# Down projection of a decoder layer: where its sums are computed, what is kept for the fourth product, and in which order its activations are loaded

## The chip, the cores and the metric

One core of one Trainium2 chip runs the whole kernel. The metric is device time in microseconds; the number of a kernel is the median of its runs. TensorE (PE in the rows) multiplies, with its weight loads listed as PEld; VectorE is DVE, ScalarE is ACT, GpSimd is POOL, and SyncE (SP) issues nearly all DMA transfers.

## The reference, cut to what matters

One decoder layer over 1024 prompt tokens and 64 sample tokens (8 sequences of 8), all in float32. The part that the change touches:

```python
    up, ffn_state = causal_dwconv(rms_norm(x, g_pre_ffn) @ w_up, ffn_prev, w_conv_f, b_conv_f)
    gate, val = jnp.split(up, 2, axis=-1)
    x = x + rms_norm((jax.nn.gelu(gate) * val) @ w_down, g_post_ffn)
    e = (p @ w_ple) * jax.nn.sigmoid(rms_norm(x, g_ple_gate) @ w_ple_gate)
    x = x + rms_norm(e, g_post_ple)
```

with d_model 1024, d_ff 2816 and a PLE width of 256. F = gelu(gate) * val is 1088 tokens by 2816 channels and w_down 2816 by 1024. Ahead of this lie the short convolution and the stick-breaking attention, which stay as they are.

## The kernel before

**Precision.** A float32 product is made of three products of rounded parts: every operand tile is rounded by ScalarE (the high part, `*oph`), VectorE subtracts that from the tile (the remainder, `*opl`), and TensorE adds high x high, low x high and high x low in PSUM.

**Seven products for eight.** For the prompt tokens F is cut into four blocks: 11 and 12 are the first 512 tokens with channels 0 to 1407 and 1408 to 2815, 21 and 22 the same of the last 512 tokens. w_down is cut alike. The kernel computes seven block products where the plain way has eight, with sums of blocks as operands. On the side of F these are S1 = 21 + 22, S2 = S1 - 11, S4 = 12 - S2 and S3 = 22 - S2; on the side of the weights T3 (22 - 12), T2 (11 + T3), T4 (21 - T2) and T1 (22 - T2). They are computed tile by tile, 128 x 512 each, in place: S1 over 21, S2 and later S3 over 11, S4 over 12, T2 over the 11 weights kept in `w1`.

**Steps.** Each product runs over k = 0 to 10 (KF = 11 tiles of 128 channels). Step s = 11 n + k is tile k of product n, so there are 77 steps (DSTEPS); the order of the products is 11 x 11, 12 x 21, S2 x T2, S3 x T3, 22 x T4, S1 x T1, S4 x 22. A step is four blocks of 128 tokens with three matmuls of 512 columns each (L3264 to L3266). In products 0, 1, 5 and 6 (steps 0 to 21 and 55 to 76) it also has two sampled matmuls ahead of the others (L3249 and L3250), with `fs`, the rounded sample columns of F.

**Order of the work.** Every engine works through its own list in order and waits on semaphores. ScalarE's loop over s from 5 has `w_high(s)`, `f_high(s)` and, at certain s, other work: `fs_high(1)` (rounds the second half of the sample columns, tile `fsraw`) at s = 7, the copies out of PSUM after products 0 and 1 at s = 12 and 23, the rounding of the gate weights (`gate_high`) at s = 60 to 62, 65, 66, and for k = 5 to 7 after the loop. VectorE's loop has `w_low(s)` and `f_low(s)` with T3's two differences and `s4_sum`, and `summed` (PSUM sums at the end of a product) at s = 34, 45, 56 and 67. The rounded tiles lie in 4 buffers for weights (NWOP) and 3 for F (NFOP): `w_high(s)` waits for the end of step s - 4, `f_high(s)` for that of step s - 3. GpSimd computes S1, S2, S3, T2, T4, T1, the remainders of the gate weights and of the PLE weights. Weight tiles arrive in a ring of 5 buffers (NR); `down_rows(s)` waits until the remainder of the tile before in its buffer is done.

T3 is computed twice: at s = 22 + k as a difference of two loaded tiles, from which T2 is made, and for product 3 as T2 minus the 11 weights, loaded a second time.

**Loads of F.** F doesn't fit into SBUF while it is made; each of its 22 channel tiles is spilled to DRAM by `spill`, and `f_group(j)` reads groups of tiles back (F_GROUPS); a group waits until the group three before it has landed. Groups with a channel tile above 17 wait for its spill (`f_landed`). SP issues all of these and the weights in one list:

```python
            down_rows(6)
            f_group(6)
            hold(d_f, 23)
            spill(21, 1)
            down_rows(7)
            hold(p_st, NFF + 1)
            f_landed(21)
            f_group(7)
```

Of the kernel before, what the change touches and what calls it, by code (L numbers as in the profile page):

```python
# [124 lines left out]
def block_end(n, b):  # L125
# [62 lines left out]
def build(nc, inp, out, gate_spill, x1_spill, x2_spill, f_spill):  # L188
    with ExitStack() as ctx:
# [136 lines left out]
        w1 = [at(f"w1_{k}", [P, HALF], 190464 + T * k if k < 3 else R2 + 32768 + T * (k - 3)) for k in range(KF)]  # L326
        wd = [at(f"wd{j}", [P, HALF], R3 + T * j if j < 4 else 67584) for j in range(NR)]
# [199 lines left out]
        g_t1, T1_0 = g_t, 4 * NFF  # L527
        g_sa, SA0 = g_s1, 4
        g_sb, SB0 = g_s, 4
        g_sc, SC0 = g_foldm, 1  # L530
        d_sd, SD0 = d_cg, NFF
        d_td, TD0 = d_cw, 2 * NFF
# [89 lines left out]
        def _(sp):  # L622
# [261 lines left out]
            def down_rows(s):  # L884

                n, k = divmod(s, KF)
                if s >= NR:
                    if 2 * KF <= s - NR < 3 * KF:
                        hold(g_t1, T1_0 + s - NR - 2 * KF + 1)
                    else:  # L890
                        hold(d_dl, s - NR + 1)
                row_, h = ((k, 0), (KF + k, 0), (KF + k, 1), (k, 0), (KF + k, 0), (KF + k, 1), (KF + k, 1))[n]
                sp.dma_start(w1[k][:, :] if n == 0 else wd[s % NR][:, :], down_block(row_, h)).then_inc(wd_in[s % NR], 16)
                if n == 2:
                    if k >= 3:
                        hold(g_t1, T1_0 + k - 2)
                    sp.dma_start(wd12[k % 3][:, :], down_block(k, 1)).then_inc(w12_in[k % 3], 16)
# [26 lines left out]
            f_group(6)  # L924
# [87 lines left out]
        def _(pool):  # L1012
# [121 lines left out]
            def down_sum(s):  # L1134

                n, k = divmod(s, KF)
                w, b = w1[k][:, :], wd[s % NR][:, :]
                if n == 2:
                    pool.wait_ge(d_td, TD0 + k + 1)
                    g.tensor_tensor(w, w, b, ALU.add).then_inc(g_t1, 1)  # L1140
                    return
                pool.wait_ge(wd_in[s % NR], 16 * (s // NR + 1))
                pool.wait_ge(g_t1, T1_0 + k + 1)
                minus(b, b, w).then_inc(g_t1, 1)

            for k in range(KF):
                a11, a21, a22 = (fa[q][k][:, :] for q in ("11", "21", "22"))
                for q in ("21", "22"):
                    j, n = F_LANDED[q, k]
                    pool.wait_ge(f_in[j], F_IN0[j] + n)  # L1150
                g.tensor_tensor(a21, a21, a22, ALU.add).then_inc(g_sa, 1)
                pool.wait_ge(g_sa, SA0 + k + 1)
                pool.wait_ge(d_fl, k + 1)
                minus(a11, a21, a11).then_inc(g_sb, 1)
            def s3_sum(k):

                a11, a22 = fa["11"][k][:, :], fa["22"][k][:, :]
                pool.wait_ge(d_sd, SD0 + k + 1)
                pool.wait_ge(d_fl, 2 * KF + k + 1)
                minus(a11, a22, a11).then_inc(g_sc, 1)  # L1160

            for k in range(KF):
                down_sum(2 * KF + k)
                if k in (6, 9):
                    s3_sum(k // 7)
            for k in range(2, KF):
                s3_sum(k)
            for s in range(4 * KF, 6 * KF):
                down_sum(s)

            for k in range(KD):
                h, l = wgate[k]
                pool.wait_ge(a_gh, k + 1)
                minus(l[:, :], wraw[k][:, :], f(h)[:, :]).then_inc(g_wl, 1)
# [6 lines left out]
        def _(act):  # L1181
# [549 lines left out]
            def w_high(s):  # L1731
# [1660 lines left out]
```

## Time and profile before

| | us |
|---|---|
| median of 3 runs (1720.69 to 1721.9) | 1721.71 |
| the profiled execution, its time | 1724.81 |
| the profiled execution, its span | 1723.1 |
| TensorE busy in the span | 1692.3 |
| VectorE busy | 1106.5 |
| ScalarE busy | 782.2 |
| GpSimd busy | 439.9 |

The down projection lies between 1331.0 and 1590.9 us of the span. All times of rows are from this one execution, counted from the start of the span. An engine's share of busy time is a mean over stages of different kind, and idle time of an engine that others don't wait for costs nothing. A matmul's duration overlaps the next one's: matmuls of 512 columns of 0.39 us begin every 0.23 us.

### The profile page before, as it was taken

Reading aid. Unit: us, or ns where it says so; the run is one execution under the profiler, and the core shown is the slowest. Engines: PE = TensorE matmul, PEld = TensorE weight load, DVE = VectorE, ACT = ScalarE, POOL = GpSimd, SP = SyncE. Lnnn points to the kernel's source line nnn. Section 1 sums busy time; section 2 is a strip of 40 time slices with the busy share of each in tenths; the row PEclk is TensorE's granted clock in tenths of the full one; section 3 lists DMA queues with packets and bytes.
Section 4 is the critical chain, followed back from the end, with each engine's and each line's share of the span. In section 5 each row is a group of like instructions: output and inputs, shape, how many; then the busy total and the mean of one; then the engine's idle time right before and its main releaser. Section 6 shows DMA issues by size and latency. Waiting matters only on the chain.

```text
span 1723.1 us, 27761 instructions
## 1 busy us (share of the span) xinstructions
PE 1692.3 (98%) x9376; PEld 1474.3 (86%) x9376; DVE 1106.5 (64%) x1481; ACT 782.2 (45%) x1402; POOL 439.9 (26%) x337
## 2 busy tenths in 40 slices
PE   8999999999999999999999999999999798999998
PEld 7989998999899989988888888888888586887886
DVE  6265145325523647648688888888887779787566
ACT  6345244434534443235454444444444243465665
POOL 1000000000000000003365555555563726451200
PEclk9999999999999999999999999999999899999999
DMA  5312221231123115343222222222224842344343
GB/s 170 102 53 71 85 71 52 68 99 51 61 81 85 43 56 183 127 171 123 66 85 77 77 76 74 73 75 73 72 70 141 287 152 81 118 140 170 120 132 116
DMA packets 178184, 173.56 MB, mean 101 GB/s; under 512 B 16383, under 2 KB 144731, under 8 KB 178076
## 3 DMA queue, kind: packets, MB, share of 16 engines
q1 hardware_dynamic: 167130, 167.30, 30.3%
q10 hardware_dynamic: 10946, 4.91, 1.0%
q8 instruction: 57, 0.93, 0.2%
q14 instruction: 51, 0.42, 0.1%
HBM read 132.54 MB, written 39.62 MB: 100 GB/s over the span
## 4 chain that ended last, share of the span: by engine, by line
PE 90%; DVE 5%; issue 2%; DMA 1%; ACT 1%; SPq 1%; DVEq 0%; ACTq 0%
PE pair L3052 11%; PE pair L2747 9%; PE pair L2749 9%; PE pair L2748 9%; PE pair L3112 8%; PE pair L3114 8%; PE pair L3113 8%; PE pair L2701 5%; PE pair L3264 3%; PE pair L3266 3%; PE pair L3265 3%; PE pair L3121 2%; PE pair L2923 2%; PE pair L2893 2%; PE pair L2678 2%; PE pair L2676 2%
## 5 line engine op out<-in xcount | busy, mean ns | idle before, releaser
L2747 PE MATMUL pair<-xh,wh 128*128 128x384 f32 (+1 forms) x952 | 324.7, 341 | 0.0
L2749 PE MATMUL pair<-xh,wl 128*128 128x384 f32 (+1 forms) x952 | 311.2, 327 | 0.0
L2748 PE MATMUL pair<-xl,wh 128*128 128x384 f32 (+1 forms) x952 | 310.5, 326 | 0.0
L1048 POOL TENSOR_TENSOR srow<-hn,hn 128x512 f32<-128x512 f32 x8 | 12.0, 1506 | 814.1 <-DVE hn L2293 813.8
L2747 PEld LDWEIGHTS pair<-xh,wh 128*128 128x128 f32 x952 | 179.2, 188 | 4.3 <-issue 2.3
L2748 PEld LDWEIGHTS pair<-xl,wh 128*128 128x128 f32 x952 | 179.3, 188 | 0.0
L2749 PEld LDWEIGHTS pair<-xh,wl 128*128 128x128 f32 x952 | 178.7, 188 | 0.0
L3264 PE MATMUL pair<-woph,foph 128*128 128x512 f32 x308 | 123.3, 400 | 8.3 <-DVE fopl L2432 5.9
L3266 PE MATMUL pair<-woph,fopl 128*128 128x512 f32 x308 | 121.4, 394 | 0.0
L3265 PE MATMUL pair<-wopl,foph 128*128 128x512 f32 x308 | 121.3, 394 | 0.0
L1400 ACT ACTIVATE keep<-pair,bias 128x512 f32<-128x512 f32 (+4 forms) x100 | 58.2, 582 | 125.7 <-DVE pair L2146 53.6
L1960 DVE TENSOR_TENSOR wl<-raw,wh 128x1024 fp32r<-128x1024 f32 x48 | 58.8, 1224 | 75.3 <-ACT wh L1207 74.9
L2432 DVE TENSOR_TENSOR fopl<-f,foph 128x512 fp32r<-128x512 f32 x77 | 90.7, 1178 | 16.4 <-ACT foph L1761 16.3
L1761 ACT ACTIVATE foph<-f 128x512 fp32r<-128x512 f32 x77 | 48.4, 628 | 94.3 <-PE pair L3266 90.0
L3264 PEld LDWEIGHTS pair<-woph,foph 128*128 128x128 f32 x308 | 58.6, 190 | 26.2 <-issue 6.8
L2146 DVE TENSOR_TENSOR pair<-pair,far 128x128 f32<-128x128 f32 x64 | 15.1, 293 | 85.9 <-PE pair L2893 85.5
L3266 PEld LDWEIGHTS pair<-woph,fopl 128*128 128x128 f32 x308 | 58.6, 190 | 12.5
L3265 PEld LDWEIGHTS pair<-wopl,foph 128*128 128x128 f32 x308 | 58.7, 191 | 11.7
L3112 PE MATMUL pair<-bh,tch 128*128 128x512 f32 x168 | 67.2, 400 | 0.0
L3112 PE MATMUL pair<-bh,adh 128*128 128x512 f32 x168 | 65.5, 390 | 0.7 <-DVE uv L2393 0.7
L3114 PE MATMUL pair<-bh,tcl 128*128 128x512 f32 x168 | 65.6, 391 | 0.0
L3113 PE MATMUL pair<-bl,tch 128*128 128x512 f32 x168 | 65.6, 390 | 0.0
(409 smaller groups left out, 4394.3 us busy)
## 6 DMA issues: line engine op xcount, KB each, us to landing
rawp<-in_w_up SPq DMA_DIRECT2D x88, 256.0 KB, 3.8
raw<-in_w_in SPq DMA_DIRECT2D x80, 256.0 KB, 3.2
wd<-in_w_down SPq DMA_DIRECT2D x66, 256.0 KB, 2.8
f_spill<-cv SPq DMA_DIRECT2D x22, 552.0 KB, 2.8
f<-f_spill SPq DMA_DIRECT2D x44, 256.0 KB, 5.6
gat<-gate_spill SPq DMA_DIRECT2D x16, 544.0 KB, 4.5
x_spill<-x SPq DMA_DIRECT2D x16, 512.0 KB, 2.9
gate_spill<-stg SPq DMA_DIRECT2D x32, 192.0 KB, 1.9
```

Source lines behind the costliest of these rows:

```text
L2432: v.tensor_tensor(fop[s % NFOP][1][:, :], fa[F_OF[s // KF]][s % KF][:, :], f(fop[s % NFOP][0])[:, :], ALU.subtract).then_inc(d_fl, 1)
L2701: return t_.transpose(b, src, ident[0:rows, 0:rows])
L2747: t_.matmul(b, h, xhi, start=(k == 0), stop=False, skip_group_check=True)
L2748: t_.matmul(b, h, xlo, start=False, stop=False, skip_group_check=True)
L2749: ins = t_.matmul(b, l, xhi, start=False, stop=(k == KD - 1), skip_group_check=True)
L3052: ins = t_.matmul(o[:, 512 * c:512 * c + 512], x, w(t, c), start=first and i == 0, stop=last and i == 2, skip_group_check=True)
L3112: t_.matmul(o, w, x, start=n in "1675" and k == 0, stop=False, skip_group_check=True)
L3113: t_.matmul(o, w, xlow, start=False, stop=False, skip_group_check=True)
L3114: ins = t_.matmul(o, wlow, x, start=False, stop=k == KH - 1, skip_group_check=True)
L3264: t_.matmul(o, xh_[:, cols], w[0][:, :], start=n in (0, 2, 3, 5) and k == 0, stop=False, skip_group_check=True)
L3265: t_.matmul(o, xh_[:, cols], w[1][:, :], start=False, stop=False, skip_group_check=True)
L3266: ins = t_.matmul(o, xl_[:, cols], w[0][:, :], start=False, stop=k == KF - 1, skip_group_check=True)
```

## The change

All S and T sums and the remainders of the gate weights are computed by VectorE, at places of its loop that are written out; GpSimd keeps the remainders of the PLE weights. T3 is written to tiles of its own, `w3`, when it is first computed, and product 3 reads it there; the second load of the 11 weights for it falls away (`load_of` numbers the loads that are left). The groups of F are ordered anew: the 12 tiles 0 to 2 and then the second `fsraw` are the first that are read after the last spill, and the 21 and 22 tiles from 4 on come after the 12 tiles. The last three gate tiles are rounded inside the loop (s = 74 to 76), with `gate_low(7)` ahead of the last PSUM sums.

```diff
-F_GROUPS = ([[("11", k) for k in range(4)], [("11", k) for k in range(4, 8)], [("s", 0)], [("11", k) for k in range(8, KF)]]
-            + [[(q, k) for k in (2 * i, 2 * i + 1) for q in ("21", "22")] for i in range(3)]
-            + [[("12", k) for k in range(4)]]
-            + [[(q, k) for k in (2 * i, 2 * i + 1) for q in ("21", "22")] for i in range(3, 5)]
-            + [[("12", k) for k in range(4, 8)], [("21", KF - 1), ("22", KF - 1), ("s", 1)], [("12", k) for k in range(8, KF)]])
+F_GROUPS = [[("11", k) for k in range(4)], [("11", k) for k in range(4, 8)], [("s", 0)], [("11", k) for k in range(8, KF)],
+            [(q, k) for k in (0, 1) for q in ("21", "22")], [(q, k) for k in (2, 3) for q in ("21", "22")],
+            [("12", k) for k in range(3)], [("s", 1)], [("12", k) for k in range(3, 7)], [("12", k) for k in range(7, KF)],
+            [(q, k) for k in (4, 5) for q in ("21", "22")], [(q, k) for k in (6, 7) for q in ("21", "22")],
+            [(q, k) for k in (8, 9, 10) for q in ("21", "22")]]
+def load_of(s):
+    return s if s < 3 * KF else s - KF
...
@@ SyncE, the list of loads
-            f_group(6)
             hold(d_f, 23)
             spill(21, 1)
             down_rows(7)
             hold(p_st, NFF + 1)
             f_landed(21)
+            f_group(6)
+            hold(d_fs, DFS0 + 1)
             f_group(7)
             down_rows(8)
             f_group(8)
             down_rows(9)
+            down_rows(10)
             f_group(9)
-            down_rows(10)
+            down_rows(11)
             f_group(10)
-            down_rows(11)
-            hold(d_fs, DFS0 + 1)
+            down_rows(12)
             f_group(11)
-            down_rows(12)
+            down_rows(13)
             f_group(12)
-            for s in range(13, DSTEPS):
-                down_rows(s)
-                if s == 51:
+            for s in range(14, DSTEPS):
+                if s // KF != 3:
+                    down_rows(s)
+                if s == 49:
                     hold(p_dn, EACH * 4)
                     sp.dma_start(pn[:, 0:BLK, :], pp).then_inc(p_in, 16)
...
@@ GpSimd: down_sum, the S1 and S2 loop, s3_sum and the gate remainders fall away
+            pool.wait_ge(g_wl, KD)
             for k in range(2):
                 pool.wait_ge(a_eh, EH0 + k + 1)
                 minus(wl[k][:, :], raw[k][:, :], f(wh[k][:, :])).then_inc(g_wl, 1)
...
@@ ScalarE, at the end of its loop
+                if s >= 74:
+                    gate_high(s - 69)
             x2_high(1)
-            for k in range(5, KD):
-                gate_high(k)
...
@@ VectorE, the new functions (s1_sum, s3_sum, s4_sum and gate_low are of the same form)
+            def s2_sum(k):
+                dve.wait_ge(d_s1, S1_N + k + 1)
+                dve.wait_ge(d_fl, k + 1)
+                v.tensor_tensor(fa["11"][k][:, :], fa["21"][k][:, :], fa["11"][k][:, :], ALU.subtract).then_inc(d_s2, 1)
+            def t3_sum(k):
+                l = load_of(2 * KF + k)
+                dve.wait_ge(wd_in[l % NR], 16 * (l // NR + 1))
+                dve.wait_ge(w12_in[k % 3], W12_IN0 + 16 * (k // 3 + 1))
+                v.tensor_tensor(w3[k][:, :], wd[l % NR][:, :], wd12[k % 3][:, :], ALU.subtract).then_inc(d_t3, 1)
+            def t2_sum(k):
+                dve.wait_ge(d_t3, T3_N + k + 1)
+                v.tensor_tensor(w1[k][:, :], w1[k][:, :], w3[k][:, :], ALU.add).then_inc(d_t, 1)
+            def t41_sum(s):
+                l = load_of(s)
+                dve.wait_ge(wd_in[l % NR], 16 * (l // NR + 1))
+                b = wd[l % NR][:, :]
+                v.tensor_tensor(b, b, w1[s % KF][:, :], ALU.subtract).then_inc(d_t, 1)
...
@@ VectorE, its loop
             for s in range(5, DSTEPS):
                 if 0 <= s + 3 - 2 * KF < KF:
-                    weights_apart(s + 3 - 2 * KF)
-                if 0 <= s + 2 - 3 * KF < KF:
-                    t3_sum(s + 2 - 3 * KF)
+                    t3_sum(s + 3 - 2 * KF)
+                if 0 <= s + 2 - 2 * KF < KF:
+                    t2_sum(s + 2 - 2 * KF)
+                if 0 <= s + 1 - 3 * KF < KF:
+                    s3_sum(s + 1 - 3 * KF)
+                if 4 * KF <= s + 2 < 6 * KF:
+                    t41_sum(s + 2)
                 w_low(s)
                 f_low(s)
+                if s in (9, 10, 11, 12):
+                    s1_sum(s - 9)
+                    s2_sum(s - 9)
+                if 14 <= s < 21:
+                    s1_sum(s - 10)
+                    s2_sum(s - 10)
                 if KF <= s - 1 < 2 * KF:
                     s4_sum(s - 1 - KF)
...
+                if 61 <= s < 64:
+                    gate_low(s - 61)
+                if s in (66, 67):
+                    gate_low(s - 63)
+                if s >= 75:
+                    gate_low(s - 70)
             x2_low(1)
+            gate_low(KD - 1)
             summed(6, lambda b: y_half(b, 1), lambda b: y_half(b, 1))
```

## Rows read from the trace of the kernel before

**Rows 1.** The page: span, and busy time of each engine.
```profile
span 1723.1 us, 27761 instructions
...
PE 1692.3 (98%) x9376; PEld 1474.3 (86%) x9376; DVE 1106.5 (64%) x1481; ACT 782.2 (45%) x1402; POOL 439.9 (26%) x337
```

**Rows 2.** Stages: us, busy PE, PEld, DVE, ACT, POOL, then clock, DMA share, GB/s.
```profile
1341.99:1356.78 14.79, 13.66 (x58) 10.20 (x57) 14.79 (x10) 3.91 (x7) 14.48 (x10) 1.00 0.85 300
1356.78:1375.66 18.88, 9.23 (x30) 6.84 (x28) 7.71 (x8) 4.43 (x8) 14.02 (x11) 0.73 0.79 269
1375.66:1416.92 41.26, 41.26 (x183) 34.17 (x182) 32.99 (x44) 18.78 (x34) 11.70 (x7) 1.00 0.44 141
1416.92:1433.24 16.32, 16.32 (x73) 13.52 (x72) 15.63 (x17) 8.13 (x15) 10.65 (x7) 1.00 0.51 161
1433.24:1457.23 23.99, 19.17 (x74) 13.84 (x72) 23.99 (x21) 7.24 (x12) 17.26 (x11) 0.93 0.15 45
1457.23:1481.71 24.48, 24.48 (x110) 20.28 (x108) 21.41 (x29) 10.51 (x18) 7.92 (x5) 1.00 0.36 108
1481.71:1487.62 5.91, 5.69 (x26) 4.43 (x25) 5.17 (x9) 2.31 (x4) 2.58 (x2) 1.00 0.17 46
...
1552.48:1557.36 4.88, 3.44 (x15) 2.55 (x14) 4.88 (x10) 1.15 (x2) 0.00 (x0) 1.00 0.16 54
```

**Rows 3.** The long stand: waits, TensorE, chain, SP, landings of fsraw and spills, full DMA.
```profile
ACT fs L1769 <- DMA fsraw<-f_spill: 16.8, 1, 16.8
...
1369.99 0.80 PE L3249 MATMUL pair<-woph,fs 128*128 128x512 f32 x1 [9.65 <-DVE wopl L2427]
...
1342.09 5.30 DMA f_spill<-cv
...
1358.87 0.45 SPq L876 DMA_DIRECT2D fsraw<-f_spill  x1
...
DMA to landing us min/median/max: 5.8/7.3/8.7
...
f_spill<-cv SPq DMA_DIRECT2D x22, 552.0 KB, 2.8
...
1353.00:1364.00 11.00, 7.34 (x31) 5.21 (x29) 4.27 (x3) 0.00 (x0) 10.69 (x9) 1.00 1.04 387
```

**Rows 4.** VectorE and GpSimd in order of time: together, then each alone.
```profile
1339.59 2.40 DVE L2369 TENSOR_TENSOR cv<-cg,cv 128x1104 f32<-128x1104 f32 x1
...
1350.39 1.78 DVE L2427 TENSOR_TENSOR wopl<-w,woph 128x512 fp32r<-128x512 f32 x1
1352.09 1.78 DVE L2432 TENSOR_TENSOR fopl<-f,foph 128x512 fp32r<-128x512 f32 x1
...
1351.70 1.62 POOL L1048 TENSOR_TENSOR f<-f,f 128x512 f32<-128x512 f32 x1
...
1457.41 0.67 DVE L2479 TENSOR_TENSOR wd<-w,wd 128x512 f32<-128x512 f32 x1
1458.01 0.68 DVE L2427 TENSOR_TENSOR wopl<-wd,woph 128x512 fp32r<-128x512 f32 x1
...
1482.21 1.29 POOL L1048 TENSOR_TENSOR wd<-wd,w 128x512 f32<-128x512 f32 x1 [1.53 <-DMA wd<-in_w_down]
```

**Rows 5.** VectorE: a dependent pair, and F's remainder at an undisturbed step.
```profile
1331.82 1.36 DVE L2356 SCALAR_TENSOR_TENSOR cg<-ug,fw,cg 128x1104 f32<-128x1104 f32 x1
1333.22 1.37 DVE L2358 SCALAR_TENSOR_TENSOR cg<-ug,fw,cg 128x1104 f32<-128x1104 f32 x1
...
1395.57 0.69 DVE L2432 TENSOR_TENSOR fopl<-f,foph 128x512 fp32r<-128x512 f32 x1 [1.28 <-ACT foph L1761]
```

**Rows 6.** A remainder of 1024 columns, the last PSUM sums, the first gate matmul.
```profile
L1960 DVE TENSOR_TENSOR wl<-raw,wh 128x1024 fp32r<-128x1024 f32 x48 | 58.8, 1224 | 75.3 <-ACT wh L1207 74.9
...
1589.30 2.51 DVE L2464 TENSOR_TENSOR y<-pair,y 128x512 f32<-128x512 f32 x4
...
1590.91 0.62 PE L3052 MATMUL pair<-wgh,x2h 128*128 128x512 f32 x2
```

More of the change, by code:

```diff
@@ L326, in build @@
         w1 = [at(f"w1_{k}", [P, HALF], 190464 + T * k if k < 3 else R2 + 32768 + T * (k - 3)) for k in range(KF)]
+        w3 = [at(f"w3_{k}", [P, HALF], R1 + 33792 + T * k if k < 8 else 56320 + T * (k - 8)) for k in range(KF)]
         wd = [at(f"wd{j}", [P, HALF], R3 + T * j if j < 4 else 67584) for j in range(NR)]
@@ L526, in build @@
         a_eh, EH0 = a_dh, DSTEPS
[L527 to L532, printed above, removed]
+        d_s1, S1_N = g_s1, 4
+        d_s2, S2_N = g_s, 4
+        d_s3, S3_N = g_foldm, 1
+        d_s4, S4_N = d_cg, NFF
+        d_t3, T3_N = d_cw, 2 * NFF
+        d_t, T_N = g_t, 4 * NFF
         a_u2, U2_0 = a_snap, NFF
@@ L886, in down_rows @@
                 n, k = divmod(s, KF)
[L887 to L893, printed above, removed]
+                l = load_of(s)
+                if l >= NR:
+                    before = l - NR if l - NR < 3 * KF else l - NR + KF
+                    hold(*((d_t3, T3_N + before - 2 * KF + 1) if before // KF == 2 else (d_dl, before + 1)))
+                row_, h = {0: (k, 0), 1: (KF + k, 0), 2: (KF + k, 1), 4: (KF + k, 0), 5: (KF + k, 1), 6: (KF + k, 1)}[n]
+                sp.dma_start(w1[k][:, :] if n == 0 else wd[l % NR][:, :], down_block(row_, h)).then_inc(wd_in[l % NR], 16)
                 if n == 2:
                     if k >= 3:
-                        hold(g_t1, T1_0 + k - 2)
+                        hold(d_t3, T3_N + k - 2)
                     sp.dma_start(wd12[k % 3][:, :], down_block(k, 1)).then_inc(w12_in[k % 3], 16)
@@ L1132, in _ @@
             states_out(i5.at(), 1)
[L1134 to L1174, printed above, removed]
+            pool.wait_ge(g_wl, KD)
             for k in range(2):
@@ L2425, in w_low @@
                 dve.wait_ge(a_dh, s + 1)
-                src = w1[s % KF] if s // KF in (0, 2) else wd[s % NR]
+                n, k = divmod(s, KF)
+                src = w1[k] if n in (0, 2) else w3[k] if n == 3 else wd[load_of(s) % NR]
                 v.tensor_tensor(wop[s % NWOP][1][:, :], src[:, :], f(wop[s % NWOP][0])[:, :], ALU.subtract).then_inc(d_dl, 1)
@@ L2464, in summed @@
                     v.tensor_tensor(out_(b), down_bank(n, b), add(b), ALU.add).then_inc(d_dn, 1)
-            def weights_apart(k):
-                dve.wait_ge(wd_in[(2 * KF + k) % NR], 16 * ((2 * KF + k) // NR + 1))
-                dve.wait_ge(w12_in[k % 3], W12_IN0 + 16 * (k // 3 + 1))
-                b = wd[(2 * KF + k) % NR][:, :]
-                v.tensor_tensor(b, b, wd12[k % 3][:, :], ALU.subtract).then_inc(d_td, 1)
-            def t3_sum(k):
-                s = 3 * KF + k
-                dve.wait_ge(wd_in[s % NR], 16 * (s // NR + 1))
-                dve.wait_ge(g_t1, T1_0 + k + 1)
-                b = wd[s % NR][:, :]
-                v.tensor_tensor(b, w1[k][:, :], b, ALU.subtract).then_inc(d_td, 1)
@@ L2481, in s4_sum, with s1_sum @@
-            def s4_sum(k):
-                dve.wait_ge(g_sb, SB0 + k + 1)
-                dve.wait_ge(d_fl, KF + k + 1)
-                a12 = fa["12"][k][:, :]
-                v.tensor_tensor(a12, a12, fa["11"][k][:, :], ALU.subtract).then_inc(d_sd, 1)
+            def s1_sum(k):
+                for q in ("21", "22"):
+                    j, n = F_LANDED[q, k]
+                    dve.wait_ge(f_in[j], F_IN0[j] + n)
+                v.tensor_tensor(fa["21"][k][:, :], fa["21"][k][:, :], fa["22"][k][:, :], ALU.add).then_inc(d_s1, 1)
@@ new lines, in s2_sum, with s4_sum, s3_sum @@
+            def s2_sum(k):
+                dve.wait_ge(d_s1, S1_N + k + 1)
+                dve.wait_ge(d_fl, k + 1)
+                v.tensor_tensor(fa["11"][k][:, :], fa["21"][k][:, :], fa["11"][k][:, :], ALU.subtract).then_inc(d_s2, 1)
+            def s4_sum(k):
+                dve.wait_ge(d_s2, S2_N + k + 1)
+                dve.wait_ge(d_fl, KF + k + 1)
+                v.tensor_tensor(fa["12"][k][:, :], fa["12"][k][:, :], fa["11"][k][:, :], ALU.subtract).then_inc(d_s4, 1)
+            def s3_sum(k):
+                dve.wait_ge(d_s4, S4_N + k + 1)
+                dve.wait_ge(d_fl, 2 * KF + k + 1)
+                v.tensor_tensor(fa["11"][k][:, :], fa["22"][k][:, :], fa["11"][k][:, :], ALU.subtract).then_inc(d_s3, 1)
@@ L2488, in p_low, with gate_low @@
+            def gate_low(k):
+                dve.wait_ge(a_gh, k + 1)
+                v.tensor_tensor(wgate[k][1][:, :], wraw[k][:, :], f(wgate[k][0])[:, :], ALU.subtract).then_inc(g_wl, 1)
             def p_low(i):
```

10 lines of the change are left out of this document (6 added, 4 removed).

## The prediction

> **What bounds the kernel now.** I read the page first: TensorE is busy for 1692.3 of 1723.1 us and VectorE for 1106.5 [rows 1], so only TensorE's waits and the spans in which its clock falls can be won. The change touches the down projection alone, so I went to the table of stages there, with borders where steps begin [rows 2]. The reader should first look for stages in which nothing disturbs TensorE. Steps 9 to 21 took 41.26 us, 3.174 us each (a step of the sampled products); steps 22 to 27 took 16.32 us, 2.72 us each (a step without sample columns). Against these two rates the other stages are too long by:
> - steps 3 to 6: 14.79 - 4 x 3.174 = 2.09 us;
> - steps 7 and 8: 18.88 - 2 x 3.174 = 12.53 us;
> - steps 28 to 33: 23.99 - 6 x 2.72 = 7.67 us;
> - steps 43 and 44: 5.91 - 2 x 2.72 = 0.47 us;
> - step 66: 4.88 - 3.174 = 1.71 us.
>
> Together 24.47 us. Steps 34 to 42 run at the full rate, and what is left of the stage (turns, the ends of products) stays as it is.
>
> Next, what ends these waits. For steps 7 and 8 the view of waits has ScalarE idle for 16.8 us until the second fsraw lands [rows 3]. The SP rows say why it is late: SP waits for the last spill (issued 1342.09, 5.30 us on its way), then issues several groups, and fsraw only at 1358.87, the 25th transfer since 1342; it lands 8.7 us later. ScalarE's loop is strictly in order, and fs_high(1) stands in it at s = 7, so steps 8 and 9 can't be prepared. TensorE stands for 9.65 us until 1369.99, and then its sampled matmul takes 0.80 us where 0.39 is usual: the granted clock of the stage is 0.73, a mean over full speed and the lower level of 1.2 GHz after the long stand [rows 2, 3]. From landing to TensorE's next matmul are 2.4 us.
>
> For the other stages the reader lays VectorE's rows beside GpSimd's [rows 4]. While GpSimd sums, its operation takes 1.62 us or more (alone: 1.29), and VectorE's takes 1.78 us, one begun every 1.70 us. While GpSimd stands still, VectorE's takes 0.68 us, one begun every 0.60 us. The two alternate as if they shared a way to the data. In steps 3 to 6 VectorE has two remainders a step: 2 x 1.70 = 3.40 us, more than the 3.174 us of the step. In steps 28 to 33 GpSimd is busy for 17.26 us and VectorE for the whole 23.99 us [rows 2]. So what GpSimd does off the path lies on it.
>
> **The change part by part.** The S, T and gate arithmetic leaves GpSimd: 33 + 33 operations of 512 columns and 8 of 1024. All go to VectorE, which loses the eleven second T3 of its own. At the busy-state price VectorE now pays up to 1.70 - 0.60 = 1.10 us for each of its own operations that meets one of these; a sum of its own costs 0.60 us. Whether the trade pays is decided per step, by whether VectorE's operations x 0.60 stay under the step:
> - s = 5 to 8: two remainders, 1.2 of 3.17 us. The 2.09 us of steps 3 to 6 go; also the product at L2369, 2.40 us under GpSimd's sums [rows 4], returns to about 1.3, the same 1.10 less, so the last spill is issued some 1.0 us earlier.
> - s = 9 to 12: w, f, S1, S2, and S4 at 12: 4 or 5 operations. S2 waits for S1 on its own engine; the nearest such pair, the two passes at L2356 and L2358, begins 1.40 us apart for a duration of 1.36 [rows 5], so I add 0.12 us: 5 x 0.60 + 0.12 = 3.12 us, just under 3.17.
> - s = 14 to 18: the same five, 3.12 us. s = 19: six, 3.7; s = 20: seven, 4.3; s = 21 and 22: five, 3.0. Behind since s = 19: 0.5 + 1.2 + 0 + 0.3 = about 2 us. From s = 23 it is four, 2.4 of 2.72 us, and the debt is worked off.
> - How much debt is free: ScalarE rounds f of step s when step s - 3 ends (the view of time has step 14 beginning at 1394.71, ScalarE at 1394.91), VectorE's remainder is through at 1396.26 [rows 5], and step s begins two steps after the first end, so 6.35 - 1.5 = 4.8 us lie between. Two are used. No wait on TensorE.
> - s = 32 to 63: at most four with S3 and T4/T1, 2.4 of 2.72 us; the four PSUM sums at a product's end no longer start late. In steps 43/44 and 66 they did: there 0.47 and 1.71 us go, and with them all 7.67 us of steps 28 to 33 (the sum at step 33 included).
> - Gate remainders: 1024 columns, 1.22 us on VectorE (L1960 [rows 6]) for 2.4 to 2.9 on GpSimd (by tile wgl). At s = 61 to 63 four operations and this make 3.0 of 3.17 us. At s = 75 and 76 ScalarE's new pair takes 2.15 us (in the view of time two pairs begin at 1588.43 and 1590.58), so f of step 75 moves from 1578.53 to 1580.7 and its remainder ends at 1582.1; step 75 starts at 1583.6. Covered, by only 1.5 us. The last one, gate_low(7), is not covered: it stands between x2_low(1) and the final sums. These begin at 1589.30 now, two of them are done 1.28 us later, and the gate's matmuls follow at 1590.91 [rows 6]. With 1.22 us ahead of them they are done at 1591.8: 0.9 us lost.
>
> **The other order of the loads.** SP: w3 to w6 and the activations to group 5 as before; then group 6 (four tiles) isn't issued there, so the queue in front of the last spill is shorter by 1 MB. At the 387 GB/s of a full stage [rows 3] that is 2.7 us. The spill, issued at 1341.0, then takes between 2.8 us (median of all 22, [rows 3]) and the 5.3 us of now; I take 3.3, as nearly nothing is queued. Group 6, three tiles, and fsraw follow at 1344.3 and 1345.7. Landing: between 5.8 and 8.7 us [rows 3]; I take 6, since the first one had three tiles ahead too. So fsraw lands at 1352 and the 2.4 us chain ends at 1354. Step 8 is due at 1341.99 + 5 x 3.174 = 1357.9. In the likeliest case all 12.53 us go; with both upper ends (1346.3 + 1.4 + 8.7 + 2.4 = 1358.8) TensorE waits for about 1 us. Everything behind it, 4 + 4 + 4 + 4 + 6 activation tiles and w8 to w14, is 29 tiles of 0.262 MB, 7.6 MB or 20 us: landed by about 1368. Of the last ones w14 is wanted first, by ScalarE at 1368 and by TensorE at 1376.9; VectorE's first sum with a late tile, S1(4), comes at s = 14, also near 1368. The eleven T3 reloads that fall away free the queue at steps 28 to 40, where nothing waits for it: worth nothing. The pn load at s = 49 instead of 51 waits for the end of step 43 with w50 behind it; pn lands in 5.6 us (by line L946), VectorE can stand about 2 us at the sum for step 50, with 3 us left before TensorE needs step 48. Nothing.
>
> **Sum.** 24.47 - 0.9 = 23.6 us. The profiled execution took 1724.81 us (span 1723.1 [rows 1]), 3.1 above the median 1721.71. So 1701.2 for a profiled execution, 1698.1 for the median.
>
> **A price that could be another.** What is seen above is 0.68 us of duration and 0.60 us from start to start. The Trainium skill, "VectorE: DVE Perf Modes", section on the TRN2 errata, gives an fp32 tensor_tensor (N + 151)/0.96 ns, 691 ns for N = 512. The duration of the row agrees, the distance of the starts doesn't. By it the sum would be an estimated 23.2 us: s = 14 to 18 would cost 3.45 us for steps of 3.17, the mild end of rival 2. The same skill, "SBUF — State Buffer", section "Who interferes with whom", says that a VectorE instruction with two SBUF inputs and a GpSimd instruction that reads SBUF exclude one another for the whole instruction; that would allow a pair only every 1.29 + 0.68 = 1.97 us (an estimate), where the rows show 1.70. By that rule a VectorE operation slows only with a partner on GpSimd, so the time would be that of the forecast and rival 3 falls away; I leave it a small chance all the same.
>
> **Rivals.**
> 1. The wait for loads only moves. fsraw comes later than I say, or the weights behind it do: 29 tiles are still asked for in 20 us. For it: DMA is at its full rate there, and fsraw took 8.7 us in it. Against it: the waiting work has 3.8 us in hand at step 8 and more later. TensorE would stand for 2 to 8 us, at the lower clock for a part: gain 14 to 21, 1701 to 1708 us.
> 2. VectorE becomes the bound in steps 14 to 23, because operations that wait for semaphores begin 0.68 to 0.75 us apart and not 0.60. At the 0.69 us of a duration: 0.3 x 5 + 1.0 + 1.7 + 0.3 + 0.7 = 5.2 us behind for 4.8 free, 0.4 us lost; at 0.75, from s = 9 to 29 some 96 operations need 72 us where TensorE's 63 and the 5 free give 68: 4 to 5 us lost. 1698.5 to 1703 us. For it: all starts of [rows 4] are of remainders and sums whose inputs lay ready.
> 3. Slower than before. VectorE's 1.70 us isn't GpSimd's doing but that of the loads or of TensorE's reading. The 96 operations would need 96 x 1.70 = 163 us for 68: 95 us more than the forecast, about 1793 us. From 0.95 us an operation on the gain is eaten up. Against it: from 1457.41 on VectorE is fast in a stage where TensorE never stands and DMA has a share of 0.36, while at steps 28 to 33, with hardly a load (0.15), it is slow [rows 2, 4]; only GpSimd differs.
> 4. It does nothing: a second late input (rounding of w8, a held queue) sits right behind fsraw and VectorE is as full as before. 1717 to 1725 us. The chain from landing to matmul has no such wait in it.
>
> **Chances.** The forecast, within 2 us of 23.6: 0.64. Rival 1: 0.14. Rival 2: 0.12. Still more gain (the waits of steps 1 and 2 too, at most 1.5 us): 0.03. Rival 4: 0.04, Rival 3: 0.03. The likeliest case's own range is 1696 to 1700.5. The range of 8 in 10 reaches from 1695.5, where every excess is gone and nothing comes in, to 1707, nearly the end of rival 1. Faster 0.94; the same (within 0.2%, 3.4 us, about what a measurement of this kernel tells from no change) 0.03; slower 0.03.
>
> **What the changed profile would show.** TensorE without a wait from 1342 to 1402, where step 22 starts (now 1416.92); ScalarE's wait for fsraw under 4 us; all remainders of 512 columns at 0.68 to 0.70 us, none at 1.78; VectorE close to full at steps 14 to 22, still a little ahead; no row of GpSimd from 1336 until the two wl remainders; a wait of about 0.9 us on VectorE before the first gate matmul; gate matmuls from about 1567.3. Wrong would be: TensorE waiting for VectorE in steps 14 to 24 (rival 2), for DMA in steps 8 to 14 (rival 1), or a wait larger than 2 us at the start of the gate.

## The result and the profile after

| | kernel before | changed kernel |
|---|---|---|
| median, us | 1721.61 (1720.69 to 1721.9) | 1699.26 (1698.91 to 1700.53) |
| ratio | | 0.9872, interval 0.9855 to 0.989 |
| profiled execution, time / span | 1724.81 / 1723.1 | 1700.53 / 1698.8 |
| down projection: first step to first gate matmul | 1331.02 to 1590.91: 259.89 | 1328.70 to 1566.48: 237.78 |

The change saves 22.35 us; 1698.1 was predicted, in a range of 1695.5 to 1707. Of the profile's difference, 22.11 us lie in the down projection, and 2.3 us ahead of it, where both kernels are the same.

The page of the changed kernel, answering to [rows 1]:

```profile
span 1698.8 us, 27696 instructions
...
PE 1685.5 (99%) x9376; PEld 1471.6 (87%) x9376; DVE 1085.7 (64%) x1544; ACT 783.4 (46%) x1402; POOL 316.9 (19%) x263
```

GpSimd has 123 us less to do than in [rows 1], and yet VectorE, which took its work, is busy for 20.8 us less: its operations became shorter by more than their number grew.

The stages of the changed kernel with the borders of [rows 2], at the starts of steps 3, 7, 9, 22, 28, 34, 43, 45 and around step 66 (us, busy PE, PEld, DVE, ACT, POOL, then clock, DMA share, GB/s):

```profile
1339.64:1352.34 12.70, 12.70 (x58) 10.52 (x56) 6.76 (x11) 5.67 (x10) 0.00 (x0) 1.00 0.89 287
1352.34:1358.68 6.34, 6.34 (x29) 5.26 (x28) 4.77 (x8) 2.94 (x5) 0.00 (x0) 1.00 1.06 398
1358.68:1400.35 41.67, 41.63 (x183) 33.86 (x182) 37.04 (x61) 19.23 (x35) 0.00 (x0) 1.00 0.56 198
1400.35:1417.80 17.45, 17.00 (x73) 13.44 (x73) 16.56 (x28) 8.27 (x15) 0.00 (x0) 1.00 0.68 226
1417.80:1434.12 16.32, 16.32 (x74) 13.51 (x72) 13.56 (x23) 6.93 (x12) 0.00 (x0) 1.00 0.06 17
1434.12:1458.60 24.48, 24.48 (x110) 20.27 (x108) 19.05 (x31) 10.39 (x18) 0.00 (x0) 1.00 0.03 11
1458.60:1464.04 5.44, 5.44 (x26) 4.50 (x24) 4.62 (x9) 2.31 (x4) 0.00 (x0) 1.00 0.21 60
1528.90:1532.08 3.18, 3.18 (x16) 2.63 (x14) 3.18 (x6) 1.15 (x2) 0.00 (x0) 1.00 0.02 6
```

Read the first column of the table, the length of each stage, against [rows 2]: 14.79 became 12.70 (four steps of 3.174), 18.88 became 6.34, 23.99 became 16.32 (six of 2.72), 5.91 became 5.44 and 4.88 became 3.18. Two stages got longer: 41.26 to 41.67 and 16.32 to 17.45. That is a new wait of 1.55 us at steps 21 to 24 (0.42, 0.34, 0.67 and 0.12). Steps 28 to 33 show best what the change did: VectorE is busy for 13.56 of 16.32 us with 23 operations, where it needed all of 23.99 us for 21. The clock column rises with it: from 0.73 to 1.00 at steps 7 and 8, from 0.93 to 1.00 at steps 28 to 33.

The second sample load of the changed kernel, in order of time (answers to [rows 3]):

```profile
1338.67 0.34 SPq L821 DMA_DIRECT2D f_spill<-cv  x1
...
1342.40 1.28 SPq L885 DMA_DIRECT2D f<-f_spill  x3
1343.86 0.39 SPq L882 DMA_DIRECT2D fsraw<-f_spill  x1
...
1348.64 0.79 ACT L1737 ACTIVATE fs<-fsraw 128x704 fp32r<-128x704 f32 x1 [1.82 <-DMA fsraw<-f_spill]
```

The last spill is out of the way 3.7 us after its issue, fsraw is asked for at 1343.86 and lands within 4.8 us, and ScalarE waits for it 1.8 us where it waited 16.8. Step 8 begins at 1355.51, 6.9 us after that.

The new wait at steps 21 to 24 of the changed kernel, in order of time:

```profile
1370.34 0.63 ACT L1713 ACTIVATE woph<-wd 128x512 fp32r<-128x512 f32 x1 [3.47 <-DMA wd<-in_w_down]
1371.00 0.69 DVE L2396 TENSOR_TENSOR wopl<-wd,woph 128x512 fp32r<-128x512 f32 x1 [2.73 <-ACT woph L1713]
...
1372.21 0.68 DVE L2440 TENSOR_TENSOR f<-f,f 128x512 f32<-128x512 f32 x1
1372.93 0.69 DVE L2446 TENSOR_TENSOR f<-f,f 128x512 f32<-128x512 f32 x1
1373.54 0.68 DVE L2452 TENSOR_TENSOR f<-f,f 128x512 f32<-128x512 f32 x1
...
1402.58 0.68 DVE L2401 TENSOR_TENSOR fopl<-f,foph 128x512 fp32r<-128x512 f32 x1
1404.15 0.69 DVE L2465 TENSOR_TENSOR w<-wd,wdb 128x512 f32<-128x512 f32 x1 [0.89 <-DMA wdb<-in_w_down]
...
1405.97 0.68 DVE L2401 TENSOR_TENSOR fopl<-f,foph 128x512 fp32r<-128x512 f32 x1
...
1406.80 0.47 PE L3277 MATMUL pair<-woph,foph 128*128 128x512 f32 x1 [0.39 <-DVE fopl L2401]
```

The weight tile of step 14 lands only at 1370.3. From its remainder at 1371.00 VectorE has 52 operations without a gap, to 1403.2 us. S2 begins 0.72 us after the S1 that it depends on, all others 0.60 us after the one before. TensorE meets that queue at step 21, and once more at 1406.80, where it waits for the remainder begun at 1405.97.

The end of the changed kernel's down projection, in order of time (answers to [rows 6]):

```profile
1564.01 1.22 DVE L2482 TENSOR_TENSOR wgl<-wgr,wgh 128x1024 fp32r<-128x1024 f32 x1
1565.14 2.48 DVE L2433 TENSOR_TENSOR y<-pair,y 128x512 f32<-128x512 f32 x4
...
1566.48 0.73 PE L3065 MATMUL pair<-wgh,x2h 128*128 128x512 f32 x2 [0.69 <-DVE y L2433]
```

### The profile page after: what moved, and what is told of

It reads as the page before. It is cut to its first block, busy times and chain, and to the rows that moved or that the text cites. A ratio compares the mean times of both kernels' runs of the same rounds, so it can differ in the third digit from the quotient of the medians.

```text
span 1698.8 us, 27696 instructions
## 1 busy us (share of the span) xinstructions
PE 1685.5 (99%) x9376; PEld 1471.6 (87%) x9376; DVE 1085.7 (64%) x1544; ACT 783.4 (46%) x1402; POOL 316.9 (19%) x263
## 4 chain that ended last, share of the span: by engine, by line
PE 92%; DVE 4%; DMA 2%; SPq 1%; issue 1%; ACT 0%; DVEq 0%; ACTq 0%
PE pair L3065 11%; PE pair L2760 9%; PE pair L2762 9%; PE pair L2761 9%; PE pair L3125 8%; PE pair L3126 8%; PE pair L3127 8%; PE pair L2714 5%; PE pair L3277 3%; PE pair L3279 3%; PE pair L3278 3%; PE pair L3134 2%; PE pair L2936 2%; PE pair L2906 2%; PE pair L2691 2%; PE pair L2689 2%
## 5 line engine op out<-in xcount | busy, mean ns | idle before, releaser
L1527 ACT ACTIVATE tch<-tc 128x1024 fp32r<-128x1024 f32 x21 | 22.3, 1061 | 94.7 <-PE pair L3127 94.7
```

## The experiments

Three questions: do the two halves of the change (other engine, other loads) pay by themselves; is it really GpSimd that makes VectorE slow; and where do the 1.55 us at steps 21 to 24 come from. An excess is always the time over 3.174 or 2.72 us a step. Every ratio is to the kernel before as it ran beside the run in question: 1722.03 us for the first three runs and for the four sums on GpSimd, 1722.23 for the four single and joint edits at steps 21 to 24, and 1721.88 for the second profile of before, the long run on GpSimd and the two runs with the late tile.

### The loads alone

The kernel before with the changed kernel's groups and SP order; the arithmetic stays on GpSimd, and T3's second load stays.

```diff
@@ F_GROUPS: as in the changed kernel
...
-            f_group(6)
             hold(d_f, 23)
             spill(21, 1)
             down_rows(7)
             hold(p_st, NFF + 1)
             f_landed(21)
+            f_group(6)
+            hold(d_fs, DFS0 + 1)
             f_group(7)
...
```

> The kernel before with the changed kernel's order of loads alone; all sums stay on GpSimd. My theory (the 22 us are two separate parts, a late fsraw and operations that GpSimd stretches): the stand at steps 7 and 8 (12.53 us) goes, steps 3 to 6 and 28 to 33 stay as long as before, so 10 to 12 us faster than before, near 1710.5. Rival (the parts need each other: with VectorE at 1.70 us an operation the early fsraw can't be used): less than 6 us faster.

Measured: 1716.39 us (1714.97 to 1717.31), ratio 0.9965 (0.9951 to 0.9979), so only 5.6 us won. The 10 to 12 us expected were missed. The number is the rival's (less than 6), its reason holds in part: the early fsraw was used, but half of the gain was lost elsewhere. The down projection took 253.6 us, 6.3 less than 259.89. Its 12.53 us at steps 7 and 8 are gone, but others came. In order of time:

```profile
1336.85 1.56 POOL L1152 TENSOR_TENSOR f<-f,f 128x512 f32<-128x512 f32 x1 [3.41 <-DMA f<-f_spill]
1337.19 1.78 DVE L2428 TENSOR_TENSOR wopl<-w,woph 128x512 fp32r<-128x512 f32 x1
...
1343.01 0.50 PE L3265 MATMUL pair<-woph,foph 128*128 128x512 f32 x1 [2.23 <-DVE fopl L2433]
```

GpSimd's first sum began 7.6 us after the start of step 0 (1329.21), where it began 8.05 us after it in the first profile of before (1339.07). Those 0.4 us decide whether it meets the weight remainder of step 3 (1.78 us here, 0.69 there): step 3 took 4.11 us too much. Step 15 lost 1.39 us, steps 22 to 33 lost 10.8 us instead of 7.67, steps 43, 44 and 66 together 1.9. 4.11 + 1.39 + 10.8 + 1.9 = 18.2, which is 6.3 less than 24.47. The loads take one stand away, and VectorE's slow stretches take half of it back. One reason can be seen in the rows: in the kernel before, six of GpSimd's sums ran during the stand, at about 1.27 us each, and the last S2 was through 48 us after the start of step 0. Here it was through only after 56 us, in step 15, where VectorE has S4 to do as well (in order of time, GpSimd's last S2):

```profile
1383.57 1.62 POOL L1049 TENSOR_TENSOR f<-f,f 128x512 f32<-128x512 f32 x1
```

Why steps 22 to 33 lost 3 us more wasn't followed up.

### The engines alone

The changed kernel with the groups and the SP order of before; all its arithmetic is the changed kernel's.

```diff
@@ F_GROUPS: as in the kernel before
...
+            f_group(6)
             hold(d_f, 23)
             spill(21, 1)
...
-            f_group(6)
-            hold(d_fs, DFS0 + 1)
             f_group(7)
...
+            hold(d_fs, DFS0 + 1)
+            f_group(11)
...
```

> The changed kernel with the order of loads of before; the sums on VectorE, T3 kept. My theory: the stand of about 12.5 us at step 8 is there again, all other excess is gone, so 9.5 to 11.5 us faster than before, near 1711. VectorE's sums of product 0 and 1 have more time after the stand. Rival (VectorE's own sums are what the order of loads had to make room for): VectorE bound in steps 14 to 24 as well, less than 7 us faster.

Measured: 1713.73 us (1713.16 to 1714.7), ratio 0.9952 (0.9935 to 0.9969): 8.3 us won, 8.95 in the down projection (250.94 us). That is less than the 9.5 to 11.5 expected and more than the rival's 7. In order of time:

```profile
1356.48 0.44 SPq L882 DMA_DIRECT2D fsraw<-f_spill  x1
...
1365.31 0.79 ACT L1736 ACTIVATE fs<-fsraw 128x704 fp32r<-128x704 f32 x1 [18.43 <-DMA fsraw<-f_spill]
...
1367.68 0.79 PE L3261 MATMUL pair<-woph,fs 128*128 128x512 f32 x1 [12.10 <-DVE wopl L2395]
```

All excess outside steps 7 and 8 is gone. There it is 14.67 us instead of 12.53: TensorE arrives 2.09 us earlier at a landing that hasn't moved, and waits as much longer. 7.67 + 0.47 + 1.71 - 0.8 (the last gate remainder, below) = 9.05, for 8.95 measured. So the 2.09 us of steps 3 to 6 are worth something only together with the other loads. Parts alone give 6.3 and 9.0, both 22.1 to 23.6.

### The sample's rounding later

The kernel before, with nothing changed but the place of the wait: `fs_high(1)` and `fs_low(1)` at s = 10.

```diff
@@ ScalarE
-                if s == 7:
+                if s == 10:
                     fs_high(1)
...
@@ VectorE
-                if s == 7:
+                if s == 10:
                     fs_low(1)
```

> The kernel before, in which ScalarE and VectorE round the second half of the sample columns at s = 10 and not at s = 7; the loads stay as they are. My theory (fsraw landed at 1367.6 us, in a list in order, is the whole stand): step 11 wants it at about 1370, so at most 2 us of the stand remain and the kernel is 9 to 12 us faster than before. Rival (the weights and activations behind it are as late): ScalarE stands for them at steps 8 to 12, and less than 4 us are won.

Measured: 1714.42 us (1712.77 to 1718.35), ratio 0.9959 (0.9945 to 0.9973), 7.6 us won, less than the 9 to 12 expected and more than the rival's 4. TensorE in order of time, with GpSimd and VectorE ahead of it:

```profile
1336.06 1.27 POOL L1151 TENSOR_TENSOR f<-f,f 128x512 f32<-128x512 f32 x1 [3.11 <-DMA f<-f_spill]
1336.09 1.78 DVE L2432 TENSOR_TENSOR fopl<-f,foph 128x512 fp32r<-128x512 f32 x1
...
1371.02 0.50 PE L3249 MATMUL pair<-woph,fs 128*128 128x512 f32 x1 [0.52 <-DVE wopl L2427]
```

The stand of 12.53 us shrank to 2.1, at steps 10 and 11 (10.4 won), so two statements moved give nearly all that the new load order gives there. But GpSimd's first sum began at 1336.06 here, 7.3 us after step 0 (1328.72), and met one remainder more; steps 2 to 6 cost 3.2 us more than in the first profile of before. With the long stand behind them that would have been hidden; without it, it counts.

### The kernel before, once more

Unchanged; a second execution with a profile.

> The kernel before, unchanged, profiled a second time. Its one profile took 1724.81 us, 3.1 over its median, and had a down projection of 259.89 us from 1331.02. If that execution was late upstream only: the down projection starts near 1328.8 and takes 259.9 us again, with 24.5 us over the undisturbed rates. If a part of the 3.1 us was in it: 258.5 to 259.5 us. If the meeting of GpSimd's first sums with steps 2 to 4 varies, as the runs with only the loads or only the later samples suggest, steps 2 to 4 cost 0 to 4 us more or less, and the stand at step 8 takes up most of what they lose.

Measured: 1722.18 us. TensorE and ScalarE in order of time:

```profile
1342.65 0.80 PE L3264 MATMUL pair<-woph,foph 128*128 128x512 f32 x1 [2.22 <-DVE fopl L2432]
...
1365.41 0.79 ACT L1769 ACTIVATE fs<-fsraw 128x704 fp32r<-128x704 f32 x1 [14.35 <-DMA fsraw<-f_spill]
...
1367.78 0.80 PE L3249 MATMUL pair<-woph,fs 128*128 128x512 f32 x1 [7.87 <-DVE wopl L2427]
```

The down projection went from 1328.85 to 1588.27: 259.42 us, and it starts 2.2 us earlier than in the first profile. So of the 3.1 us that the first profile lay over its median, 2.2 were upstream and 0.5 here. Inside, the parts differ: step 3 lost 4.04 us (GpSimd's first sum began at 1336.46, 7.6 us after step 0), steps 7 and 8 10.71. 14.75 us together, 14.62 in [rows 2]. The sum is stable because the stand ends when fsraw lands, whatever was lost before it. Steps 63 and 66 together lost 1.08 us, where step 66 alone had lost 1.71.

### GpSimd beside VectorE: sums, copies, memsets

The changed kernel with work on GpSimd that no result uses: 4 memsets, 4 copies, 4 sums of 128 x 512.

```diff
@@ SyncE, at s == 64
+                    hold(g_self, G0 + 12)
...
@@ GpSimd
+            t5, t6, t7 = (fa["11"][k][:, :] for k in (5, 6, 7))
+            pool.wait_ge(p_dn, step_end(44))
+            for _ in range(4):
+                then(g.memset(t7, 0.0))
+            pool.wait_ge(p_dn, step_end(47))
+            for _ in range(4):
+                then(g.tensor_copy(t7, t5))
+            pool.wait_ge(p_dn, step_end(50))
+            for _ in range(4):
+                then(g.tensor_tensor(t7, t5, t6, ALU.add))
             pool.wait_ge(g_wl, KD)
```

> The changed kernel with 12 extra GpSimd operations of 512 columns on a free tile beside VectorE's steps 46 to 55: four memsets (no SBUF input), four copies (one), four adds (two). My theory (the two engines share a way for SBUF reads): VectorE's remainders and sums take 0.68 us beside the memsets, up to 1.8 beside the copies and the adds; its sums out of PSUM change little; the time changes by less than 2 us. Rival (any GpSimd work slows VectorE): slow beside the memsets too. Rival (only two inputs collide): 0.68 us beside the copies.

Measured: 1699.14 us. GpSimd's four sums and VectorE beside them, in order of time:

```profile
1480.35 6.79 POOL L1153 TENSOR_TENSOR f<-f,f 128x512 f32<-128x512 f32 x4 [5.79 <-PE pair L3292]
...
1481.61 1.00 DVE L2409 TENSOR_TENSOR wopl<-wd,woph 128x512 fp32r<-128x512 f32 x1 [0.71 <-ACT woph L1726]
1482.53 1.76 DVE L2414 TENSOR_TENSOR fopl<-f,foph 128x512 fp32r<-128x512 f32 x1
1484.22 0.54 DVE L2502 TENSOR_TENSOR pl<-pair,ph 128x384 fp32r<-128x384 f32 x1
```

1.76 us is back in a stage where VectorE's differences of 512 columns took 0.68: this refutes rival 3 directly, since loads and TensorE are what they were. The operation with a source in PSUM (0.54 us, as beside the memsets: 0.55) isn't slowed. Few VectorE operations ran beside the memsets, so a second run had 24 memsets and 12 copies.

> The changed kernel with work on GpSimd that no result uses: 24 memsets of 128 x 512 from the end of step 44, 12 copies of 128 x 512 from the end of step 51. If GpSimd slows VectorE only where both read SBUF: VectorE's 512-column differences stay at 0.67 to 0.70 us beside the memsets, and beside the copies many of them take more, up to 1.8 us, while its sums and remainders with a PSUM source stay as they are. If any GpSimd instruction takes part of VectorE's time: 0.9 us or more beside the memsets too. TensorE loses nothing at 0.7 to 1.1 us an operation, since VectorE has at most four of them in a step of 2.72 us: down projection 236.2 us, 1699 us.

Measured: 1699.04 us, the same. GpSimd's rows, then VectorE's:

```profile
1462.79 13.95 POOL L1147 MEMSET f<- 128x512 f32 x24 [129.82 <-PE pair L3289]
...
1468.11 0.69 DVE L2411 TENSOR_TENSOR fopl<-f,foph 128x512 fp32r<-128x512 f32 x1
...
1483.35 11.28 POOL L1150 COPY f<-f 128x512 f32<-128x512 f32 x12 [6.61 <-PE pair L3289]
1484.65 0.92 DVE L2406 TENSOR_TENSOR wopl<-wd,woph 128x512 fp32r<-128x512 f32 x1 [0.77 <-ACT woph L1723]
1485.50 1.09 DVE L2411 TENSOR_TENSOR fopl<-f,foph 128x512 fp32r<-128x512 f32 x1
1486.52 0.48 DVE L2499 TENSOR_TENSOR pl<-pair,ph 128x320 fp32r<-128x320 f32 x1
```

Beside the memsets all of VectorE's differences stay at 0.68 to 0.69 us. Beside copies, which read one tile, they take 0.69 to 1.10, not up to the 1.8 that both expectations allowed; beside sums, which read two, up to 1.76. So what counts is that GpSimd reads, and how much, not that it runs. The Trainium skill, "SBUF — State Buffer", section "Who interferes with whom", ties the exclusion to GpSimd instructions that read SBUF; the memsets agree with it. Exclusion for a whole instruction is more than the rows show: a copy alone takes 0.62 us and an operation beside copies grows by at most 0.42 us; a sum alone takes 1.26 to 1.29 us and an operation beside sums grows by 1.08.

### Steps 21 to 24

Three single edits of the changed kernel, and all three together. The weight tile of step 14 asked for ahead of the last group of activations:

```diff
             down_rows(13)
+            down_rows(14)
             f_group(12)
-            for s in range(14, DSTEPS):
+            for s in range(15, DSTEPS):
```

> The changed kernel; SyncE asks for w14 ahead of the last group of six activation tiles instead of behind it. Theory A (VectorE is late at steps 21 to 24 by 1.55 us because ScalarE stood 3.47 us for w14 and VectorE 2.73 us with it, when it had work for nearly every step behind that): the stand for w14 falls under 1 us, of the 1.55 us at most 0.4 stay, 1.1 to 1.5 us faster than the changed kernel. Theory B (the number of VectorE's operations from s = 19 alone): the 1.55 us stay within 0.3.

The S4 sums out of the full stretch, to steps 31 to 41:

```diff
-                if KF <= s - 1 < 2 * KF:
-                    s4_sum(s - 1 - KF)
+                if 31 <= s < 31 + KF:
+                    s4_sum(s - 31)
```

> The changed kernel; VectorE computes S4 at s = 31 to 41 instead of 12 to 22, so s = 14 to 18 have four operations of 512 columns and s = 20 six. Both theories have the wait at steps 21 to 24 go, as VectorE then makes up 0.6 us a step: 1.3 to 1.6 us faster than the changed kernel; no new wait at steps 32 to 43, four operations in 2.72 us. A rival: the PSUM sums at step 34 start late and cost up to 1 us there.

The last gate remainder behind the final sums:

```diff
-            gate_low(KD - 1)
             summed(6, lambda b: y_half(b, 1), lambda b: y_half(b, 1))
+            gate_low(KD - 1)
```

> The changed kernel; the last gate remainder (1.22 us on VectorE) stands behind the final PSUM sums instead of ahead of them. The stand of 0.69 us before the first gate matmul goes, nothing else: 0.6 to 0.8 us faster than the changed kernel. Rival (ScalarE's or the turns' ends set that start): no change.

> The changed kernel with all three edits: w14 earlier, S4 later, last gate remainder behind the sums. The excess of steps 21 to 24 (1.55 us) and the 0.69 us at the gate go and nothing else does: 2.1 to 2.3 us faster than the changed kernel, 24.5 us faster than before.

| kernel | median, us | ratio (interval) | down projection, us | excess at steps 21 to 24 |
|---|---|---|---|---|
| changed | 1699.26 (1698.91 to 1700.53) | 0.9872 (0.9855 to 0.989) | 237.78 | 1.55 |
| tile of step 14 earlier | 1699.11 (1698.69 to 1699.43) | 0.9865 (0.9848 to 0.9881) | 236.3 | 0 |
| S4 later | 1699.75 (1699.08 to 1700.9) | 0.9871 (0.9854 to 0.9887) | 236.3 | 0 |
| last gate remainder later | 1698.23 (1698.01 to 1700.09) | 0.9863 (0.9847 to 0.988) | 235.4 | 0 |
| all three | 1699.0 (1697.88 to 1700.19) | 0.9863 (0.9846 to 0.9879) | 235.4 | 0 |

None of the times can be told from the changed kernel's; the gains of 0.6 to 2.3 us that were expected don't show in the medians. The first two profiles seemed to confirm both remedies. But the third, whose order up to the end is the changed kernel's, had no excess either, nor had the two runs with work on GpSimd. In the third, in order of time:

```profile
1368.40 0.63 ACT L1713 ACTIVATE woph<-wd 128x512 fp32r<-128x512 f32 x1 [1.51 <-PE pair L3279]
...
1564.11 0.61 PE L3065 MATMUL pair<-wgh,x2h 128*128 128x512 f32 x2
```

Here the tile was rounded at 1368.40, not 1370.34, with the stage starting at the same time. So the excess belonged to one of four profiles with this order, the slowest execution of its kernel, and the two remedies had shown nothing. What the third does show is the price of the last gate remainder: the first gate matmul no longer waits for VectorE, and the stage is 0.8 us shorter.

To make the late tile happen every time, the load of step 14 was held back until step 11 ends, once with the changed kernel's order on VectorE and once with S4 later as well (the diff shows the hold alone, S4 is moved as above):

```diff
+            hold(p_dn, step_end(11))
             for s in range(14, DSTEPS):
```

> The changed kernel with the load of the weight tile of step 14 held back until step 11 ends. In the changed kernel's profile that tile was rounded at 1370.34 us and TensorE lost 1.55 us in steps 21 to 24; in two other profiles with the same order it was rounded at 1368.40 and 1368.91 and nothing was lost there. Theory A (a late tile of step 14 plus a VectorE that is full from step 14 on): step 11 ends at 1368.2, the landing takes 2.2 to 3.0 us, so the tile is rounded at 1370.4 to 1371.2, VectorE works without a gap from there to step 22, and TensorE loses 1.6 to 2.4 us in steps 21 to 24; down projection 237.8 to 238.6 us, median 1700.5 to 1701.5. Theory B (the loss in the one profile came from something else, a semaphore's or a load's hiccup near step 21): nothing in steps 21 to 24, 236.2 us, median 1699.0.

> As the run before, and the eleven S4 sums are moved from steps 12 to 22 to steps 31 to 41. Theory A: VectorE has four operations (2.5 us) instead of five (3.12) in steps 14 to 18 and works off the late start, so steps 21 to 24 lose nothing (under 0.3 us): 236.2 us, median 1699.0 to 1699.5. If the late tile alone made TensorE wait, whatever VectorE has to do, the loss stays at 1.6 to 2.4 us as in the run before. If the S4 sums crowd their new place, steps 31 to 42 run over 2.72 us each.

Measured: 1701.85 us (1701.12 to 1703.51), ratio 0.9883 (0.9867 to 0.99), against 1698.95 us (1698.88 to 1699.19), ratio 0.9868 (0.9852 to 0.9885). The two spreads don't touch; the first median is 0.35 us above the 1700.5 to 1701.5 expected. The first, in order of time:

```profile
1373.60 0.63 ACT L1714 ACTIVATE woph<-wd 128x512 fp32r<-128x512 f32 x1 [4.34 <-DMA wd<-in_w_down]
...
1399.96 0.50 PE L3263 MATMUL pair<-woph,fs 128*128 128x512 f32 x1 [0.62 <-DVE wopl L2397]
```

The second, its only row for it:

```profile
1371.27 0.63 ACT L1714 ACTIVATE woph<-wd 128x512 fp32r<-128x512 f32 x1 [4.43 <-DMA wd<-in_w_down]
```

The second's stage starts 2.4 us earlier, so both tiles are rounded 3.3 us before step 14 begins. With S4 in its place TensorE lost 2.15 us in steps 20 to 24 (238.4 us), without it nothing (236.2 us). Laid out by how long before step 14 its tile is rounded: 6.2, 6.0 and 5.8 us, no loss; 4.2 us, 1.55 us lost; 3.3 us, 2.15 us lost; 3.3 us with S4 later, none. Both are needed, a late tile and a full VectorE. Of the 2.9 us between the medians, 0.75 are not in the stages of these profiles, and what they are stays open.

## Why the prediction was right

**The sum.** The five excesses were priced at 24.47 us and all of them are gone; 0.9 us was predicted for the last gate remainder and 0.8 measured (237.8 - 1.55 = 236.2 us with it ahead of the sums, 235.4 behind them). 24.47 - 0.8 - 1.55 = 22.12 us, 22.11 in the profiles. Without the 1.55 us, in five other profiles with the last gate remainder in its place, the down projection takes 236.2 to 236.3 us: 23.6 us below the first profile of before, as forecast, and 23.1 below the second. The 1.2 us by which the median is over the forecast are no failed term of the stage. The forecast carried the whole difference to the profiled execution's 1724.81 over to the median, and took off a 23.6 that holds against that execution and is 0.5 less against the other. The rest of it isn't resolved; seven profiles of the changed kernel and of its variants with this load order agree within 0.2 us on where the stage begins (1328.7 to 1328.9), two others begin 1.9 to 2.4 us later. So it is partly chance that the profiled execution, 1700.53 us, came so near the 1701.2 forecast for it: 1.55 us lost in the stage were made up for by 2.3 us ahead of it.

**Steps 7 and 8.** Right, with the terms somewhat off: the spill took 3.7 us (3.3 assumed), fsraw's landing 4.8 (6). Counted as in the prediction, with 2.4 us from landing to matmul (1348.64 + 2.4 = 1351.0, for a step that begins at 1355.51), the reserve at step 8 was 4.5 us rather than 3.8. The load order was half of the case only: its run alone won 6.3 us of 12.53, because the prediction's list has the losses of the kernel before, which the stand had partly covered.

**GpSimd.** The price of a meeting, 1.10 us for 0.60, was read from rows of one kernel and came back when sums were put on GpSimd again (1.08 us more for an operation). Rival 3 fell.

**The count on VectorE.** 0.60 us an operation and 0.12 for the dependent S2 were both met: 52 x 0.60 + 7 x 0.12 = 32.0 us for the 32.2 from 1371.00 to 1403.2. The sign that the prediction gives for rival 2, TensorE waiting for VectorE in steps 14 to 24, did show in the profiled execution, with 1.55 us. Of rival 2, the place was right and the reason wrong: not the distance of the starts filled the reserve, but a load. The step that failed is "w14 is wanted first, by ScalarE at 1368": it was taken to have landed by then, which in the time of the changed profile is 1365.7; it was rounded between 1368.4 and 1370.3 in the four profiles with this order. From its remainder on VectorE has 42 operations up to those of step 21, 42 x 0.60 + 7 x 0.12 = 26.0 us, in which TensorE does seven steps, 22.2 us. So the remainder must, by this estimate, begin 3.8 us before step 14. It began 3.55 us before it in the changed kernel's profile and 2.7 in the run with the load held back, but 5.1 to 5.5 us before it in the three profiles without a loss. The reserve was counted from s = 19, as if VectorE came there with no debt; a load that is late at s = 14 is a debt which five operations a step can't work off. A second part came later: at 1404.15 VectorE waited 0.89 us for a wdb tile, and 0.79 of the 1.55 us are lost after it. The tile was asked for only at 1398.11, since SP's list stood until 1396.72 for a weight buffer that VectorE's remainder of step 21 (begun at 1395.95) frees. The third run has the same wait, 1.06 us at 1402.39, and loses nothing by it; there SP's list went on 1.9 us earlier, at 1394.80. So by itself this wait cost nothing; it added to the loss where VectorE was already behind.

**The rest.** T3's reloads, pn, the gate weights at s = 61 to 76: no excess anywhere after step 24, so nothing as predicted. Steps 34 to 42 took 24.48 us with the reloads and without them. Rival 1 happened in a form that costs 0 to 1.55 us, not 2 to 8; rival 4 didn't.

## What to carry to other kernels

Work given to an idle engine isn't free if it reads SBUF beside a busy one: compare an operation's duration with the helper running and standing, and move the work back if its sum at the undisturbed price fits the step. A stand that ends at a fixed landing hides every loss ahead of it, so two halves of a change are to be priced together: here 6.3 and 9.0 us alone, and 22.1 to 23.6 together. And before a remedy for a wait is believed, look whether the wait is there in a second execution; if it comes and goes, make it happen each time and then take it away.

## What was new about the chip

GpSimd's memsets of 128 x 512 (0.58 us from start to start) cost VectorE nothing, its copies up to 0.42 us an operation, its sums 1.1 us, and VectorE operations with a PSUM source were spared by all three (0.54 to 0.55 us for 384 columns). VectorE begins independent operations of 512 columns every 0.60 us though each is listed with 0.68; one that needs the result before it begins 0.72 us after it. And how much such a meeting costs hangs on tenths: GpSimd's first sum began 7.3 to 8.05 us after step 0 in four profiles with the old arithmetic, in three of them as its tile landed, and the loss of steps 2 to 6 (2.8, 4.7, 4.8 and 5.9 us) differed by 2 to 3 us with it.
